# An expert layer on one Trainium2 core: pairs of token and expert sorted into 32-slot tiles, with the weights read in a fixed order

## The reference, cut to what matters

```
def _moe_sublayer(x, ...):
    ht = _rms(x, ffn_norm_g).reshape(B * S, D)
    g_prob = jax.nn.softmax((ht @ w_router_group).astype(jnp.float32) + b_router_group, axis=-1)
    p_group, g_sel = lax.top_k(g_prob, 1)
    e_logit = ((ht @ w_router_expert) + b_router_expert).reshape(T, N_EXPERT_GROUPS, EXPERTS_PER_GROUP)
    e_logit = e_logit[jnp.arange(T), g_sel[:, 0]]
    top_val, top_idx = lax.top_k(e_logit, TOP_K_EXPERTS)
    w_top = jax.nn.softmax(top_val, axis=-1) * p_group
    expert_id = g_sel * EXPERTS_PER_GROUP + top_idx
    combine = jnp.sum(jax.nn.one_hot(expert_id, N_EXPERTS) * w_top[..., None], axis=1)
    for e in range(N_EXPERTS):
        hid = jax.nn.silu(ht @ w_expert_gate[e]) * (ht @ w_expert_up[e])
        y = y + combine[:, e:e + 1] * (hid @ w_expert_down[e])
    return x + y.reshape(B, S, D)
```

## Time and profile before

| | us |
|---|---|
| median of 3 runs | 3041.74 (3039.63 to 3041.78) |
| the profiled execution: its own time | 3040.31 |
| its span in the trace | 3038.3 |
| TensorE busy | 2987.3 (98% of the span) |
| VectorE busy | 2158.0 (71%) |
| ScalarE busy | 1244.6 (41%) |

### The profile page before, as it was taken

The page is one execution under the profiler, slowest core; times in us unless marked ns, Lnnn a source line. Parts: engine busy times, 40 slices in busy tenths (PEclk is TensorE's granted clock), DMA queues, the critical chain, the costliest instruction groups (busy, mean ns, idle before and its releaser), DMA issues.

```text
span 3038.3 us, 41386 instructions
## 1 busy us (share of the span) xinstructions
PE 2987.3 (98%) x15914; PEld 2418.1 (80%) x15914; DVE 2158.0 (71%) x3963; ACT 1244.6 (41%) x2153; POOL 133.6 (4%) x217
## 2 busy tenths in 40 slices
PE   8999999999999999999999999999999999999998
PEld 7777778888888888878887888888888788876665
DVE  4576876778787866577667876767765777657776
ACT  4322323423222323232336554545444545436664
POOL 0000000000000000000000000000201110001002
PEclk9999999999999999999999999999999999999999
DMA  9778784354555455548546764556666444659997
GB/s 366 279 263 290 280 274 132 125 180 159 181 167 180 160 184 169 179 148 278 181 150 226 253 209 144 177 171 200 192 232 194 146 141 146 194 182 383 352 344 288
DMA packets 189732, 645.58 MB, mean 212 GB/s; under 512 B 21840, under 2 KB 30160, under 8 KB 189536
## 3 DMA queue, kind: packets, MB, share of 16 engines
q1 hardware_dynamic: 126368, 420.03, 40.4%
q10 hardware_dynamic: 58320, 208.17, 20.2%
q0 software_dynamic: 4848, 14.75, 1.5%
HBM read 626.09 MB, written 14.68 MB: 211 GB/s over the span
## 4 chain that ended last, share of the span: by engine, by line
PE 90%; DVE 5%; ACT 2%; DMA 1%; issue 1%; POOL 0%; SPq 0%; POOLq 0%; DVEq 0%; ACTq 0%
PE PS L502 14%; PE PS L498 11%; PE PS L500 9%; PE PS L501 9%; PE PS L631 7%; PE PS L633 7%; PE PS L632 7%; PE PS L1500 2%; PE PS L1515 2%; PE PS L1057 2%; PE PS L1516 2%; PE PS L1517 2%; PE PS L794 2%; DVE WL L2424 1%; PE PS L1115 1%; PE PS L1095 1%
## 5 line engine op out<-in xcount | busy, mean ns | idle before, releaser
L2424 DVE TENSOR_TENSOR WL<-WR,WH 128x1024 fp32r<-128x1024 f32 (+1 forms) x566 | 682.4, 1211 | 401.0 <-ACT WH L1605 399.7
L502 PE MATMUL PS<-HT,WL 128*128 128x256 f32 (+1 forms) x2928 | 951.3, 325 | 0.0
L1605 ACT ACTIVATE WH<-WR 128x1024 fp32r<-128x1024 f32 (+1 forms) x566 | 587.1, 1044 | 869.0 <-PE PS L502 471.6
L502 PEld LDWEIGHTS PS<-HT,WL 128*128 128x128 f32 x2928 | 552.5, 189 | 47.8 <-issue 0.5
L498 PE MATMUL PS<-HT,WH 128*128 128x512 f32 x1584 | 565.6, 401 | 9.4 <-DVE WL L2424 6.3
L500 PE MATMUL PS<-HT,WH 128*128 128x512 f32 (+1 forms) x1344 | 518.4, 386 | 5.1 <-DVE HT L2404 2.4
L501 PE MATMUL PS<-HT,WH 128*128 128x512 f32 (+1 forms) x1344 | 507.8, 378 | 0.0
L631 PE MATMUL PS<-WH,HT 128*128 128x512 f32 x1016 | 408.8, 402 | 3.5 <-DVE HT L2404 2.5
L633 PE MATMUL PS<-WH,HT 128*128 128x512 f32 x1016 | 396.9, 391 | 0.0
L632 PE MATMUL PS<-WL,HT 128*128 128x512 f32 x1016 | 396.3, 390 | 0.0
L498 PEld LDWEIGHTS PS<-HT,WH 128*128 128x128 f32 x1584 | 298.0, 188 | 89.2 <-issue 14.0
(11 more groups left out here) (483 smaller groups left out, 3676.0 us busy)
## 6 DMA issues: line engine op xcount, KB each, us to landing
WR<-ada_w SPq DMA_DIRECT2D x264, 512.0 KB, 4.8
WR<-m_vo ACTq DMA_DIRECT2D x64, 512.0 KB, 4.3
WR<-a_qz ACTq DMA_DIRECT2D x64, 512.0 KB, 5.1
WR<-n_m SPq DMA_DIRECT2D x64, 512.0 KB, 4.6
AR<-ada_p ACTq DMA_DIRECT2D x56, 512.0 KB, 6.5
AR<-ada_p SPq DMA_DIRECT2D x48, 512.0 KB, 7.7
WR<-e_gu SPq DMA_DIRECT2D x45, 512.0 KB, 7.1
YT<-e_gu SPq DMA_DIRECT2D x44, 512.0 KB
```

The source lines that it names most:

```text
L502: return e.matmul(ps[:, 0:b - a], wl, HH_[:, c, a:b], start=False, stop=c == last)
L1605: e.activation(part_of(WH, s), place_of(plan["slot"][p])[:, 0:width(s)], ACT.Copy, scale=1.0).then_inc(*L.up(hi_done, ("hi", s)))
L2424: e.tensor_tensor(part_of(WL, s), place_of(plan["slot"][plan["split"][s]])[:, 0:width(s)], part_of(WH, s).bitcast(F32), ALU.subtract).then ...
```

## The change

The expert layer works by **pairs** of token and expert. There are 512 pairs. They are sorted by expert and laid into tiles of 32 slots: tiles 0 to 15 are static, tile j holding the first 32 pairs of expert j; what an expert has beyond 32 goes into the 16 dynamic tiles, whose expert is known only at run time (`E_ORD`). A selection matrix with 1024 columns in two halves (`E_P`; half 0 for the static, half 1 for the dynamic tiles) picks the rows with products (`pick`, L1379): four fp32r matmuls of 512 columns for each of 16 blocks of the width and each half.

The weights are read in a **fixed order**: 24 rounds u of 4 MiB, 8 DMAs of 512 KB each (`load_expert`, L3852), with all 16 experts' share in each round; rounds 0 to 15 are gate/up, 16 to 23 down. They land in one of two regions (`AR` and `E_RING`), from u = 16 on in one of three (also `E_XS`). A region is loaded anew when the static tiles have used it (`e_static`) and when the copies out of it are made (`e_copied`). Nothing is cut into high and low: `static_up` (L1400) and `dynamic_up` are plain fp32 matmuls with a stationary of 128x32, four experts at a time in the four quarters of the columns, 512 columns wide. For the dynamic tiles ScalarE copies eight and VectorE eight 128x512 pieces of each round from the region into `E_DYN`, from an address in a register (`copies`), so that TensorE's addresses are fixed.

`down` (L1437) is the same with 256 columns; its result in slots is cut into high (ScalarE, `high_out`) and low (VectorE, `low_out`) and brought back to tokens by products with a matrix of zeros and ones, `join_slots` (L1451), four fp32r matmuls of 256 columns with a full stationary. A sum over the tokens' two pairs comes out of that by itself. The residual is added in `finish`, and plain transfers store the result, in place of the indirect scatters. `late` brings the softmax factors into the slots' order with 32 small fp32 matmuls. The first round is loaded in the out-projection before the layer, the second once the last block of x has been turned. In the out-projection ScalarE and VectorE also split the rows (`low_rows`), a copy and a subtraction per block.

```diff
+    def landing(u):
+        return E_ROUND[region_of(u)]
+
+    def dead_before(u):
+
+        if u < 2:
+            return [("full", ("no", 7)) if u == 0 else "x_dead"]
+        if u == 18:
+            return ["gu_done"]
+        v = u - 2 if u < 18 else u - 3
+        return [("e_static", v), ("e_copied", v)]
+
+    def pieces(u, which=range(8)):
+        return [("E", u, i) for i in which]
+
+    def sorted_rows(half, c, j):
+
+        at = 256 * (1 - half) + 32 * (j % 8)
+        return E_XS[:, j // 8, c, at:at + 32]
...
-+            def pick(c, half):
+                ps = bank(4 + turn["pick"] % 4, ("pk", c, half))
+                turn["pick"] += 1
+                w.wait_ge(L.at(("P", half), ("rowl", c)))
+                for n, (x, tb) in enumerate(itertools.product((HH_, HL_), range(2))):
+                    m = e.matmul(ps[:], x[:, c, 128 * tb:128 * tb + 128], E_P[tb][:, 512 * half:512 * half + 512],
+                                 start=n == 0, stop=n == 3)
+                m.then_inc(*L.up(mm_done, ("full", ("pk", c, half))))
...
+            def static_up(u):
+                for g in range(4):
+                    ps = bank(g, ("e_gu", g)) if u == 0 else place[("e_gu", g)]
+                    w.wait_ge(L.at(*pieces(u, (2 * g, 2 * g + 1)), ("e_xs", 0, u)))
+                    for j in range(4 * g, 4 * g + 4):
+                        lane = 32 * (j % 4)
+                        m = e.matmul(ps[lane:lane + 32, :], sorted_rows(0, u, j), landing(u)[:, 512 * j:512 * j + 512],
+                                     start=u == 0, stop=u == 15)
+                    names = ([("e_static", u)] if g == 3 else []) + ([("full", ("e_gu", g))] if u == 15 else [])
+                    if names:
+                        m.then_inc(*L.up(mm_done, *names))
+
+            def dynamic_up(u):
+                for g in range(4):
+                    ps = bank(4 + g, ("e_gu", 4 + g)) if u == 0 else place[("e_gu", 4 + g)]
+                    w.wait_ge(L.at(*(("e_dyn", u, j) for j in range(4 * g, 4 * g + 4)), ("e_xs", 1, u)))
+                    for j in range(4 * g, 4 * g + 4):
+                        lane = 32 * (j % 4)
+                        m = e.matmul(ps[lane:lane + 32, :], sorted_rows(1, u, j), E_DYN[:, 512 * j:512 * j + 512],
+                                     start=u == 0, stop=u == 15)
+                    names = [("dyn_used", u, g)]
+                    if u == 15:
+                        names += [("full", ("e_gu", 4 + g))] + (["gu_done"] if g == 3 else [])
+                    m.then_inc(*L.up(mm_done, *names))
...
+            def down(q, b):
+                u = 16 + q
+                ps = bank((2, 3, 0, 1, 4, 5)[(8 * q + b) % 6], ("slots_out", q, b))
+                half, g = divmod(b, 4)
+                w.wait_ge(L.at(("e_hs", half), *(pieces(u, (2 * g, 2 * g + 1)) if half == 0 else
+                                               [("e_dyn", u, j) for j in range(4 * g, 4 * g + 4)])))
+                source = E_DYN if half else landing(u)
+                for k in range(2):
+                    for l in range(4):
+                        at = 512 * (4 * g + l) + 256 * k
+                        m = e.matmul(ps[32 * l:32 * l + 32, 0:256], E_HT[:, k, 128 * b + 32 * l:128 * b + 32 * l + 32],
+                                     source[:, at:at + 256], start=k == 0, stop=k == 1)
+                names = [("full", ("slots_out", q, b))]
+                if b == 3:
+                    names.append(("e_static", u))
+                elif half:
+                    names.append(("dyn_used", u, g))
+                m.then_inc(*L.up(mm_done, *names))
+
+            def join_slots(q, b):
+                ps = bank(6 + q % 2, ("e_out", q)) if b == 0 else place[("e_out", q)]
+                w.wait_ge(L.at(("place", b), ("out_low", q, b)))
+                for part in range(2):
                     for tb in range(2):
+                        m = e.matmul(ps[:, 256 * tb:256 * tb + 256], E_PT[:, b, 128 * tb:128 * tb + 128],
+                                     E_Y[(8 * q + b) % 4][part], start=b == part == tb == 0, stop=b == 7 and part == tb == 1)
+                m.then_inc(*L.up(mm_done, ("joined", q, b), *([("full", ("e_out", q))] if b == 7 else [])))
...
-                for t in tiles:
-                    ranks = ((0,), (0, 2), (1,))[t]
-                    ps = bank_of(i, t) if k == 0 else banks[t]
-                    w.wait_ge(L.at(("lo", plan["moe"][i][ranks[-1]], k)))
-                    if t == 1 and plan["ready"]:
-                        wh, wl = (W[:, bass.DynSlice(second, 1), n].rearrange("p a n -> p (a n)") for W in (WH, WL))
-                    else:
-                        wh, wl = (W[:, SLOT_OF[ranks[0]], n] for W in (WH, WL))
-                    hi, lo = operands(i, t, k)
-                    e.matmul(ps[:], hi, wh, **first, stop=False)
-                    e.matmul(ps[:], hi, wl, start=False, stop=False)
-                    j = e.matmul(ps[:], lo, wh, start=False, **last)
...
+            turn["pick"] = 0
+            for c in range(NB):
+                pick(c, 0)
+                if c:
+                    pick(c - 1, 1)
+                if c == 3:
+                    static_up(0)
+                elif c == 9:
+                    static_up(1)
+                elif c == 12:
+                    late()
+                    turn["pick"] += 1
+            pick(15, 1)
+            dynamic_up(0)
+            static_up(2)
+            dynamic_up(1)
+            dynamic_up(2)
+            for u in range(3, 16):
+                static_up(u)
+                dynamic_up(u)
+            turn_hidden(0)
+            waiting = []
+            for q in range(8):
+                for b in range(8):
+                    down(q, b)
+                    waiting.append((q, b))
+                    if (q, b) < (0, 3):
+                        continue
+                    if (q, b) == (0, 3):
+                        turn_hidden(1)
+                        continue
+                    for _ in range(2):
+                        if len(waiting) > 2:
+                            join_slots(*waiting.pop(0))
+            for q, b in waiting:
+                join_slots(q, b)
...
+            def copies(u, which):
+                for j in which:
+                    w.wait_ge(L.at(*pieces(u), *([("dyn_used", u - 1, j // 4)] if u else [("full", ("out", "nsa", 15))])))
+                    source = landing(u).rearrange("p (n m) -> p n m", m=512)
+                    if plan["ready"]:
+                        source = source[:, bass.DynSlice(experts[j], 1), :].rearrange("p a m -> p (a m)")
+                    e.activation(E_DYN[:, 512 * j:512 * j + 512], source, ACT.Copy, scale=1.0).then_inc(
+                        *L.up(act_done, ("e_dyn", u, j), ("e_copied", u)))
...
-                    split(x)
+                elif c == 6:
+                    copies(0, high_half)
+            for u in range(1, 16):
+                copies(u, high_half)
+            for b in range(4):
+                tanh(b)
+            hidden_in(0)
+            for b in range(4, 8):
+                tanh(b)
+            hidden_in(1)
+            for q in range(8):
+                for b in range(8):
+                    high_out(q, b)
+                    if b < 4:
+                        copies(16 + q, (8 + 2 * b, 9 + 2 * b))
...
+                if tag == "nsa" and n > 1:
+                    for j in (0, 1) if n == 2 else (n - 1,):
+                        low_rows(j)
...
+                if tag == "nsa" and 1 <= n <= 8:
+                    order("expert", n - 1)
...
+            low_half = range(8)
+            late_0()
+            for c in range(NB):
+                rows_in(c)
+                if c < 8:
+                    know(c)
+                elif c == 8:
+                    copies(0, low_half)
+                elif c == 9:
+                    late_1()
+                elif c == 11:
+                    scales()
+            for u in range(1, 16):
+                copies(u, low_half)
+            for b in range(4):
+                values(b)
+            hidden_in(0)
+            for b in range(4, 8):
+                values(b)
+            hidden_in(1)
+            for q in range(8):
+                for b in range(8):
+                    low_out(q, b)
+                    if b < 2:
+                        copies(16 + q, range(4 * b, 4 * b + 4))
+                    elif b == 2 and q:
+                        finish(q - 1)
+            finish(7)
...
+            elif kind == "expert":
+                load_expert(0, x[0])
+            elif kind == "experts":
+                for u in range(1, NU):
+                    for i in range(8):
+                        load_expert(u, i)
+                    if u == 18:
+                        w.wait_ge(L.at(("rows", "stored")))
+                        for tb in range(2):
+                            e.dma_start(E_RES[:, :, tb, :], XT[128 * tb:128 * tb + 128].rearrange(
```

(41 more changed lines are left out.)

707 lines of the change are left out of this document (217 added, 490 removed).

## The result

| | us | against before |
|---|---|---|
| before | 3040.27 median of 14 (3037.50 to 3041.83) | |
| changed | 3049.82 median of 14 (3043.15 to 3053.61) | 1.0031 [1.0023, 1.0039] |

The forecast was 3040, no difference; the time lies in the range, but the difference is clear and its sign was not forecast. The profiled execution is one of the longer ones (3053.28, span 3051.5). Executions of the changed kernel lie 10 us apart, those of the one before 4 (in its later, longer sets of runs 9); the fastest, 3043.15, has a mean granted clock of 0.997, the others 0.991 to 0.996.

What follows compares the result with a forecast made beforehand. Whole kernel bound by TensorE; in the expert layer, memory bounds rounds 3 to 15 (to 2911.2), TensorE the down products (+121, to 3032.2). The end gives 3036.1, span 3036.5; plus 2.0 and 1.4, 3040 us; range 3018 to 3068.

Steps and rivals of the forecast that it cites:

- A: Stretch from TensorE's first pick to its first dynamic set; forecast 45.3 us.
- B: Stretch from TensorE's first dynamic set to its first down product; forecast 153.9 us.
- C: Stretch from TensorE's first down product to its last join; forecast 110.0 us.
- step 2: Picks and first rounds: 29.1 us of picks, 7.2 of `late`, static rounds 6.9; round 3's load at about 2776.
- step 4: Down products: TensorE bounds them at 1.67 us per product with join, memory is ahead; +121 us, ending at 3032.2.
- Routing: Start of the expert layer: longer VectorE chain puts the first pick at 2723.0, 3.9 us later than before.
- Rival C: Rounds 3 to 15: TensorE's waits lower its clock; up to 44 us, so 3084, or 3062 at half; chance 0.10.
- Rounds 3 to 15: Later gate/up rounds: bound by memory at 408 GB/s, 10.28 us each, ending at 2911.2.
- Rival B: Weight stream runs at 356 GB/s, not 408, adding 19.5 us for 3060; chance 0.15.
- rival E: Copies into `E_DYN` bound the rounds, 20 us more for 3060; chance 0.07.
- rival A: Down stage: changes of shape cost nothing, or memory binds from 2911 on; 3020; chance 0.22 including 3012 to 3034.
- D: Four lanes of matmuls don't run wholly beside each other; bounds nothing to 55 us, given as 3054; chance 0.08.

Runs made afterwards that it cites:

- e7: Changed kernel with the 32 small matmuls of `late` left out but for one, so softmax factors are wrong; 3038.7 us, 0.9996 against before.
- e2: Changed kernel with VectorE's addition of the residual five outputs later; 3048.4 us, 1.0026 against before.
- e6: Changed kernel with the small matmuls of `late` moving 63 columns instead of 3; 3046.0 us, 1.0025 against before.
- e8: Changed kernel with wide small matmuls, round 1's static tiles behind the first dynamic ones, joins two by two and later residual addition together; 3032.7 us.
- e4: Changed kernel with the static tiles of round 1 behind the first dynamic tiles instead of among the picks; 3048.1 us, 1.0026 against before.
- e9: The kernel of e8 with ten idle 128x128 fp32 transposes in TensorE's wait ahead of the fifth down product; 3031.2 us, 0.9976 against before.

## Why the prediction was wrong

Its sum against the profile comes out in three parts: A 7.1 us too short, B 1.0, C 6.7, and 0.8 in the routing. Together that is the 15.6 us by which the last join started later in this execution (3047.84 against 3032.2). By the medians the sum is 9.8 us too short.

Two steps failed. The first is the price of `late` and of the picks behind it, taken at full clock in step 2 (4.9 us in the profile, and 3.5 to 4 by e7's ratio and median). The second is "memory is ahead" in step 4 (6.1 us in the profile, 1.4 by the medians of e2). So the experiments account for a good half of the 9.8; the rest is read from single profiles.

1. *Routing*: right. First pick at 2723.84, forecast 2723.0, and 0.5 of the 0.8 lies ahead of the chain, which begins at 2712.23. The 0.2 us a step holds for the longer chain.
2. *Picks and first rounds*: **this is the step that failed first**, in one term. `late` was costed at 0.11 a record in the full clock and the picks at 0.227; the small matmuls brought the clock down, which cost 2.3 us in `late` and 2.6 in the picks, shown by e6 and e7. The remaining 2.2 are mostly the wait of 1.82 for ScalarE's copy of a pick, behind its eight copies of round 0 (2740.82 to 2745.08), where 0.3 was counted; it is 1.82 in all ten profiles, and no experiment removed it. Rival C looked for the lower clock only in rounds 3 to 15, where TensorE waits. There it fell too (0.93 from 2800 to 2840), and it cost nothing, since memory bounds them: B is 155.2 us in e8, where it didn't fall there, and 155.9 in e4, where it fell six times. It had been overlooked that TensorE's clock can fall while the engine is busy without a gap.
3. *Rounds 3 to 15*: right. 10.2 us each at 408 to 409 GB/s, ended by landings; B is 154.9 to 156.1 us in all ten kernels (153.9 forecast), whatever the clock did in them. By the Trainium skill, "DMA: Bandwidth & Descriptors", section "Where 436 GB/s comes from", the memory's side binds at about 358 GB/s for a core. The trace of this program, which runs on one core alone, doesn't agree: it has 408 to 409 GB/s in the windows from 2800 to 2860. Rival B and rival E fell.
4. *Down*: the mechanism and the 1.67 are right, so rival A fell, and so did D: a set of four lanes of 512 columns takes 0.86, as long as a set of two in the earlier trace rows (0.43 for one of its two passes). The Trainium skill, "TensorE: Matmul & The Clock Gate", section "Measured speedup vs the span model", has 2.38 times for three tiles side by side. Here four lanes give four times: the ten full-width fp32 transposes of 128 columns in e9 take 2.40 us, 0.24 each, so a full-width product of 512 columns would take some 0.9, an estimate, and the set of four takes no longer. What failed is "memory is ahead": true of the weights, not of the residual, whose transfer stands behind them in the same queue. That put a wait of 3.6 us on the path, and the clock at half behind it (2.5 us more).
5. *End*: right, 3.4 us from the last join to the end of the span, where 3.9 were summed. The sum's 3036.1 becomes a span of 3036.5 without a word on the 0.4. What was priced at 0 to 10 us in the out-projection cost 0.5 at most in this execution, since the routing begins 0.5 later than before.

The overlooked terms all have one sign, and so has the error: this sum took durations read at full clock and too few waits, so it came out as a lower bound.

What stays open is where the clock falls from one execution to the next. The changed kernel's median is 3.5 us under the profiled execution. Over the first four down products the clock was at half for a part in all nine experiments' profiles (5.0 to 6.6 us for the four) and not in the changed kernel's (3.7), where it fell behind the wait of 2.55 us just after them. What would hold the clock through the start of the down products wasn't found.

## What to carry to other kernels

Price small matmuls on the path with what they do to TensorE's clock and to the wide ones behind them; if they must stand there, give them more columns to move where these are free. Do work of one stationary shape together: 0.33 us for each way there and back was 21 us in 64 turns (64 x 0.33). And look in a queue for the one small transfer that the first consumer waits for: all the weights ahead of it count.

## What the runs showed of the hardware that was not expected

TensorE's granted clock fell from 1.00 to 0.50 while the engine was busy without a gap, in fp32 matmuls of 3 columns that start every 0.11 us, in five of five profiles; with 63 columns at the same pace it stayed at 1.00, in four of four. Matmuls of 63 and of 3 columns take the same time there. A mix of such small matmuls with wide ones, after the clock had fallen, kept it at 0.50 for 24 us, where an unmixed row of wide ones saw it rise again after 5.1 us. In rounds where TensorE waited a third of the time the clock fell now and then, mostly for 3.4 us at a time, and rose by itself.
